# Gated outputs laid by token tile, and output products run between the gated steps, in a one-core decoder layer

## The reference

```
def hybrid_mixer(u, w_in, w_a2, b_a, b_f, g_gla, w_out):
    ...
    o_fox = fox_attention(fq.reshape(shp), fk.reshape(shp), fv.reshape(shp), log_f)
    ...
    o_gla = gla_chunked(...)          # o_intra + o_inter, per chunk of 64 tokens
    o_gla = rmsnorm(o_gla, g_gla.reshape(GLA_HEADS, GLA_HEAD_V)).reshape(B, S, GLA_VW)
    o_gla = o_gla * jax.nn.silu(gr)
    return jnp.concatenate([o_fox, o_gla], axis=-1) @ w_out
```

## Time and profile before

| | |
|---|---|
| median of 3 runs | 1203.12 us (1202.19 to 1206.01) |
| time of the profiled execution | 1202.4 us |
| its span, first to last instruction | 1200.7 us |
| TensorE busy | 1162.8 us, 97% |
| VectorE, ScalarE, GpSimd busy | 30%, 37%, 39% |
| mean granted clock of TensorE | 0.994 |

### The profile page before, as it was taken

The page is one execution under the profiler, slowest core; times in us unless marked ns, Lnnn a source line. Parts: engine busy times, 40 slices in busy tenths (PEclk is TensorE's granted clock), DMA queues, the critical chain, the costliest instruction groups (busy, mean ns, idle before and its releaser), DMA issues.

```text
span 1200.7 us, 14983 instructions
## 1 busy us (share of the span) xinstructions
PE 1162.8 (97%) x5565; PEld 963.0 (80%) x5565; DVE 355.6 (30%) x713; ACT 445.9 (37%) x728; POOL 472.7 (39%) x216
## 2 busy tenths in 40 slices
PE   8999999999999999999899999799999999999998
PEld 6888888888888778788678878678888888888886
DVE  3131221310006264655546104516213122130003
ACT  5232232322126455454535534425523223232213
POOL 2344354354442542222224753122543434435441
PEclk9999999999999999999999999899999999999999
DMA  6232323232322222111223442022332333323233
GB/s 197 88 105 87 105 87 105 88 105 88 105 90 69 88 88 71 53 53 54 71 70 117 146 142 88 18 71 71 93 101 94 98 97 95 100 93 104 90 102 109
DMA packets 83835, 110.91 MB, mean 92 GB/s; under 512 B 8718, under 2 KB 53836, under 8 KB 83788
## 3 DMA queue, kind: packets, MB, share of 16 engines
q1 hardware_dynamic: 83696, 110.24, 28.1%
q10 hardware_dynamic: 92, 0.02, 0.0%
HBM read 108.14 MB, written 2.10 MB: 92 GB/s over the span
## 4 chain that ended last, share of the span: by engine, by line
PE 67%; issue 19%; POOL 8%; DVE 4%; ACT 1%; DMA 1%; SPq 0%; POOLq 0%; DVEq 0%; ACTq 0%
PE bank L1397 22%; PE bank L1401 22%; PE bank L1398 22%; POOL w_lo L566 7%; DVE h L1050 1%; DVE tmp L1039 1%; DMA raw<-in_ffn_w_gu 1%; ACT w_hi L622 0%; POOL q_hi L604 0%; POOL q_lo L604 0%; DVE pt_lo L1170 0%; DVE xl L1002 0%; PE bank L1418 0%; PE bank L1421 0%; DVE smax L1144 0%
## 5 line engine op out<-in xcount | busy, mean ns | idle before, releaser
L566 POOL TENSOR_TENSOR w_lo<-raw,w_hi 128x1024 fp32r<-128x1024 f32 x193 | 461.5, 2403 | 707.5 <-ACT w_hi L622 695.2
L1397 PE MATMUL bank<-xh,w_hi 128*128 128x512 f32 (+1 forms) x920 | 353.3, 384 | 5.2 <-POOL w_lo L566 2.6
L1401 PE MATMUL bank<-xl,w_hi 128*128 128x512 f32 (+1 forms) x920 | 351.8, 382 | 0.0
L1398 PE MATMUL bank<-xh,w_lo 128*128 128x512 f32 (+1 forms) x920 | 351.7, 382 | 0.0
L622 ACT ACTIVATE w_hi<-raw 128x1024 fp32r<-128x1024 f32 x196 | 204.5, 1056 | 361.3 <-DMA raw<-in_ffn_w_down 169.3
L1397 PEld LDWEIGHTS bank<-xh,w_hi 128*128 128x128 f32 x920 | 173.0, 188 | 40.3 <-issue 3.9
L1401 PEld LDWEIGHTS bank<-xl,w_hi 128*128 128x128 f32 x920 | 173.1, 188 | 33.9
L1398 PEld LDWEIGHTS bank<-xh,w_lo 128*128 128x128 f32 x920 | 173.2, 188 | 32.2
L1397 PE MATMUL bank<-w_hi,mid_hi 128*128 128x512 f32 x352 | 137.3, 390 | 0.0
L1398 PE MATMUL bank<-w_hi,mid_lo 128*128 128x512 f32 x352 | 137.0, 389 | 0.0
L1401 PE MATMUL bank<-w_lo,mid_hi 128*128 128x512 f32 x352 | 137.0, 389 | 0.0
(11 more groups left out here) (227 smaller groups left out, 1168.6 us busy)
## 6 DMA issues: line engine op xcount, KB each, us to landing
raw<-in_ffn_w_gu SPq DMA_DIRECT2D x176, 256.0 KB, 2.9
raw<-in_ffn_w_down SPq DMA_DIRECT2D x88, 256.0 KB, 2.8
raw<-in_mix_w_in SPq DMA_DIRECT2D x48, 256.0 KB, 2.8
raw<-in_mem_w_kv SPq DMA_DIRECT2D x32, 256.0 KB, 3.1
raw<-in_mix_w_out SPq DMA_DIRECT2D x16, 256.0 KB, 2.8
raw<-in_mem_w_q SPq DMA_DIRECT2D x16, 256.0 KB, 3.0
raw<-in_mem_w_o SPq DMA_DIRECT2D x16, 256.0 KB, 2.9
h<-in_x SPq DMA_DIRECT2D x4, 512.0 KB, 5.3
```

What stands on the lines that cost most here:

```text
L566: gp.tensor_tensor(w_lo[:, n % SLOTS, :], raw[:, n % SLOTS, :], w_hi[:, n % SLOTS, :].bitcast(F32), ALU.subtract).then_inc(lo_ready, 1)
L1397: pe.matmul(dst, w[0], x[0], start=start, stop=False, skip_group_check=loose)
L1398: pe.matmul(dst, w[1], x[0], start=False, stop=False, skip_group_check=loose)
L1401: return pe.matmul(dst, w[0], x[1], start=False, stop=stop, skip_group_check=loose)
```

## The change

- The gated outputs of token tile m, all four heads, go to one bank (`gla_tile(m)`: bank 6 for even m, 7 for odd), and are squared and copied tile by tile inside the loop. Banks 4 and 5 are free from the start.
- The products with the state are cut in two: heads 0 and 2, then, after a wait for them (even_done), heads 1 and 3.
- FoX products of token tile 0 run earlier: block 0 ahead of the last FoX output, blocks 1 to 3 between the gated steps, three products at a time. Those of token tile 1 stay behind the steps.
- The key turns move ahead of the last FoX output, and their saving with them. The warm-up product is gone.
- Head sums are made per token: the squares of a head and tile are the weights, one column of ones is streamed, and the results are 16 columns of bank 0. Root and reciprocal work on 128 x 16. The spread makes four products of 128 columns a head in place of one of 512.

```
+            def square(m):
+                act.wait_ge(o_done, m + 1)
+                act.activation(tmp[:, :, m * P:(m + 1) * P], gla_tile(m), ACT.Square).then_inc(gsq, 1)
...
-                rms_root(tmp[:, 3, :], bank[0][:, :], GLA_V).then_inc(groot, 1)
+                rms_root(g_root[:, :], bank[0][:, 0:GLA_H * TC], GLA_V).then_inc(groot, 1)
...
+                def copy(m):
+                    dve.wait_ge(gsq, m + 1)
+                    dve.tensor_copy(o_sb[:, :, m * P:(m + 1) * P], gla_tile(m)).then_inc(gcopy, 1)
...
                     step(2 * m - 1)
                     step(2 * m)
-                dve.wait_ge(mem_root_s, 1)
-                dve.reciprocal(mem_rinv[:, :], mem_root[:, :]).then_inc(mem_inv, 1)
+                    if m == 2:
+                        dve.wait_ge(mem_root_s, 1)
+                        dve.reciprocal(mem_rinv[:, :], mem_root[:, :]).then_inc(mem_inv, 1)
+                    copy(m - 1)
+                copy(TC - 1)
...
-                dve.reciprocal(tmp[:, 3, :], tmp[:, 3, :]).then_inc(ginv, 1)
+                dve.reciprocal(g_rinv[:, :], g_root[:, :]).then_inc(ginv, 1)
...
+                    if phase == FOX and k == len(units) + late:
+                        fox_rows_out(0, 0)
+                        turn_ke()
...
+            def fox_rows_out(c, t, half=(0, 1)):
+
+                pe.wait_ge(y_l, 2 * c + 2)
+                free = {}
+                if c == 0:
+                    free = {0: (in_tmp, 13), 1: (in_tmp, 14)} if t == 0 else {2: (gcopy, 3), 3: (gcopy, 4)}
+                rows_block(1, B_OUT + c, fox_rows(c), c == 0, free=free, ms=tuple(2 * t + i for i in half), used=False)
...
+                    from_state(m, 0).then_inc(even_done, 1)
+
+                def from_state(m, e):
+
                     for n in (2 * m, 2 * m + 1):
                         if n:
                             tok = slice(n * CHUNK, (n + 1) * CHUNK)
-                            for hd in range(GLA_H):
+                            part = slice(n % 2 * CHUNK, (n % 2 + 1) * CHUNK)
+                            for hd in (e, e + 2):
                                 c, r, cols = head(hd)
-                                last = pe.matmul(bank[4 + hd][:, tok], state[r, n - 1, cols], gq[r, c, tok],
+                                last = pe.matmul(gla_tile(m)[:, hd, part], state[r, n - 1, cols], gq[r, c, tok],
                                                  start=False, stop=n % 2 == 1, skip_group_check=True)
...
+                def odd_outputs(m):
+
+                    pe.wait_ge(even_done, m + 1)
+                    from_state(m, 1).then_inc(o_done, 1)
+
+                def sums(m):
+
+                    pe.wait_ge(gsq, m + 1)
+                    for hd in range(GLA_H):
+                        last = pe.matmul(bank[0][:, hd * TC + m:hd * TC + m + 1], tmp[:, hd, m * P:(m + 1) * P],
+                                         ones[:, 0:1], start=hd == m == 0, stop=True, skip_group_check=True)
+                    return last
+
+                def spread_head(hd):
+                    if hd >= 2:
+                        pe.wait_ge(gfactor, hd - 1)
+                    for t in range(TC):
+                        last = pe.matmul(bank[1 - hd % 2][:, t * P:(t + 1) * P],
+                                         g_rinv[:, hd * TC + t:hd * TC + t + 1].to_broadcast([P, P]), ident[:, :],
+                                         start=True, stop=True)
+                    last.then_inc(gspread, 1)
+
...
-                pe.wait_ge(y_l, Y_FOX)
-                warm_up(bank[2], 1)
                 scores(0)
                 chunk_state(0)
                 for m in range(TC):
...
                         scores(m + 1)
                         chunk_state(2 * m + 1)
                         chunk_state(2 * m + 2)
+                        fox_rows_out(m + 1, 0, (0,))
                     outputs(m)
+                    if m + 1 < TC:
+                        fox_rows_out(m + 1, 0, (1,))
+                    else:
+                        for j in range(TC - 1):
+                            sums(j)
+                    odd_outputs(m)
...
-                pe.wait_ge(y_l, Y_FOX)
-                fox_out(0)
-                fox_out(1)
-                fox_out(2)
-                sums().then_inc(gstat, 1)
                 mem_turn(0)
-                fox_out(3)
-                fox_out(4)
+                sums(TC - 1).then_inc(gstat, 1)
+                fox_rows_out(0, 1)
+                fox_rows_out(1, 1)
                 pe.wait_ge(ginv, 1)
                 spread_head(0)
                 spread_head(1)
-                fox_out(5)
+                fox_rows_out(2, 1)
                 mem_turn(1)
-                fox_out(6)
                 spread_head(2)
                 spread_head(3)
-                fox_out(7)
+                fox_rows_out(3, 1)
```

More of the change, by code:

```diff
@@ L58 @@
 LEAD = 3
-SUM_ROWS = P // GLA_H
 TAU = 16.0
@@ L369, in build @@
         st_ready = sem("st_ready")
+        even_done = sem("even_done")
         o_done = sem("o_done")
@@ L884, in gla @@
                 act.preload_act_table(ACT.Sqrt)
+                act.wait_ge(in_hi, 20)
+                square(0)
                 act.wait_ge(mem_landed, 16 * MC)
@@ L891, in gla @@
                 rms_root(mem_root[:, :], mem_ms[:, :], D).then_inc(mem_root_s, 1)
+                square(1)
                 act.wait_ge(mem_inv, 1)
@@ L895, in gla @@
                                    scale=mem_rinv[:, t:t + 1]).then_inc(mem_normed, 1)
-                act.wait_ge(o_done, TC)
-                for hd in range(GLA_H):
-                    act.activation(tmp[:, hd, :], bank[4 + hd][:, :], ACT.Square).then_inc(gsq, 1)
+                    square(2 + t)
                 def mem_hi_chunks(cs):
@@ L1733, in fox_rows, with turn_ke @@
                 return fox_hi[:, c, :], fox_lo[:, c, :]
+            def fox_rows_out(c, t, half=(0, 1)):
[4 more added lines that the diff above has]
+                rows_block(1, B_OUT + c, fox_rows(c), c == 0, free=free, ms=tuple(2 * t + i for i in half), used=False)
+            def turn_ke():
+                pe.wait_ge(gdec, 3)
+                pe.wait_ge(expd, N_FOX)
+                for t in range(2):
+                    for j in range(4):
+                        m, c = 2 * t + j // 2, j % 2
+                        last = pe.transpose(bank[t][:, j * P:(j + 1) * P], gke[:, c, m * P:(m + 1) * P],
+                                            ident[:, :])
+                    last.then_inc(ke_turned, 1)
             def gla():
@@ L1820, in mem_turn @@
                             last.then_inc(mem_turned, 1)
-                def fox_out(q):
-                    c, t = q // 2, q % 2
-                    free = {2 * t + half: (gcopy, q * 2 + half + 1) for half in range(2)} if c == 0 else {}
-                    rows_block(1, B_OUT + c, fox_rows(c), c == 0, free=free, ms=(2 * t, 2 * t + 1), used=False)
-                def sums():
-                    for hd in range(GLA_H):
-                        pe.wait_ge(gsq, hd + 1)
-                        rows = slice(SUM_ROWS * hd, SUM_ROWS * (hd + 1))
-                        last = pe.matmul(bank[0][rows, :], ones[:, 0:SUM_ROWS], tmp[:, hd, :],
-                                         start=True, stop=True)
-                    return last
-                def spread_head(hd):
-                    if hd >= 2:
-                        pe.wait_ge(gfactor, hd - 1)
-                    row = SUM_ROWS * hd
-                    pe.matmul(bank[1 - hd % 2][:, :], ident[:, row:row + 1].to_broadcast([P, P]), tmp[:, 3, :],
-                              start=True, stop=True).then_inc(gspread, 1)
-                pe.wait_ge(y_l, Y_FOX)
-                fox_out(0)
-                fox_out(1)
-                fox_out(2)
-                sums().then_inc(gstat, 1)
                 mem_turn(0)
-                fox_out(3)
-                fox_out(4)
+                sums(TC - 1).then_inc(gstat, 1)
+                fox_rows_out(0, 1)
+                fox_rows_out(1, 1)
                 pe.wait_ge(ginv, 1)
```

30 lines of the change are left out of this document (14 added, 16 removed).

## The result

| | before | after |
|---|---|---|
| median of 5 runs each | 1203.24 us (1202.19 to 1206.01) | 1208.86 us (1207.32 to 1210.66) |
| profiled execution: time, span | 1202.4, 1200.7 us | 1207.51, 1205.8 us |
| mean granted clock of TensorE | 0.994 | 0.992 |

The ratio is 1.0043, 95% interval 1.0026 to 1.006. The kernel became 5.6 us slower, where +1.6 was forecast, and its median lies just outside the range. Ratios go by the means of the runs; where runs fall into two groups, the median can stand elsewhere, so both are given.

A forecast was written before the change was run, and what follows sets the result against it. TensorE was taken as the bound, working 1162.8 of 1200.7 us. Gains of 5.0 us against costs of 6.6 gave net +1.6 us on the median of 1203.12, so 1204.7 us, range 1200.8 to 1208.4.

The forecast's parts named there:

- The front, the waits: Front, end of gated steps, before spreads: waits go, gaining 2.7, 1.7 and 0.6 us; new mask wait of 0.7 us.
- State products and changes of mode: Gated steps: one-half state products at 0.107 us a step cost 3.0 us; 64-row/128-row switches cost 1.1 us.
- Head sums: Behind squares of gated outputs: 32 weight loads at 0.107 us, 3.4 us less the old 1.0, cost 2.4 us.
- the wait for ginv: Before the spreads: reciprocal on 16 columns instead of 512, with 12 products covering it, removes the wait, gain 0.6 us.
- Sum of the work: Whole stretch: gains 5.0, costs 6.6, net +1.6 us; second token half at 614.5 instead of 612.9; chance 0.47.
- The clock falls in the sums: Rival, behind last tile's inner products: mostly weight loads bring half clock, +3.3 us, 1206.4; second fall 1208.1; chance 0.30.

The follow-up runs named there:

- The reorderings alone: Kernel before with key turns and memory turns moved earlier, no warm-up product, old-form sums behind six FoX products: 1198.16 us, ratio 0.9961.
- fourth experiment: Kernel before with only the order of its state products changed: heads 0 and 2, then 1 and 3; 1203.98 us, ratio 1.0011.
- the four lines above: Stretch times of changed kernel, its repeat, sums directly behind turns, sums behind six FoX products: 47.42, 45.87, 45.86, 44.30 us with 10.24, 6.83, 6.83, 3.42 at half clock.
- sixth experiment: Kernel before with only the one-column head sums and their root, reciprocal and spreads: 1205.36 us, ratio 1.0014.
- third experiment: Changed kernel with the old head sums, root, reciprocal and spreads put back: 1202.55 us, ratio 1.0001.
- tenth: Changed kernel with all 32 sum instructions in one row behind the memory turns and six FoX products: 1204.56 us, ratio 1.0019.
- first: Changed kernel with one 512-column dummy product behind each of the three early groups of head sums: 1215.36 us, ratio 1.0072, in two groups.
- seventh: Changed kernel with nine FoX products of token tile 1 moved among the early sums: 1206.7 us, ratio 1.0043, in groups.
- ninth: Changed kernel with five full products of FoX data, result unused, behind each of the three early head sums: 1213.93 us, ratio 1.0074.

## Why the prediction was wrong, step by step

- **The front, the waits.** Right: scores(1) at 578.73 with 0.69 us on the mask (579 and 0.7 forecast), no wait behind the steps nor ahead of the spreads. The reorderings alone confirm that these gains are real: 3.6 us in the stretch, 5 in the time.
- **State products and changes of mode.** Steps of 0.107 as forecast for eight in a row (1.03 us with a mode change), no pairs. From scores(1) to the memory turns the changed kernel takes 603.14 - 578.73 = 24.4 us; less 24 sums (2.6), 18 FoX products (4.1) and what the half clock cost (0.6) that is 17.1, where the kernel before takes 593.24 - 580.33 = 12.9. So these two terms are 4.2 together, 3.0 + 1.1 forecast. Right. In the kernel before the same split costs 1.5 (fourth experiment), because its halves overlap; here FoX products or sums stand between them. Only the odd products of two tiles meet the next scores, and little is saved by it:

```profile
589.41 0.77 PE L1832 MATMUL bank<-gq,state 64*128 64x64 f32 x5
...
590.35 0.66 PE L1790 MATMUL bank<-gq,gk 64*128 64x128 f32 x5
590.85 1.13 PE L1806 MATMUL bank<-gv,gla_a 64*128 64x256 f32 x8
```

Eight state products and eight scores take 590.85 - 589.41 = 1.44 us, against 1.03 and, in the kernel before, 0.51 (587.35 to 587.86) apart.

- **Head sums.** 0.109 us a load, 3.49 for 32: right as work, and +1.7 to +2.2 us alone with their spreads (2.5 forecast, less the 0.6 of the wait for ginv, is 1.9). The Trainium skill's price for a product of one column (TensorEngine Tiling (Array Packing), section Instruction Overhead), some 0.8 us in all as the prediction's estimate, doesn't hold with full weight loads: the trace has 3.49.
- **Sum of the work.** 42.3 us for the stretch without the half clock (47.42 - 5.1), or 42.7 by the four lines above; 42.4 forecast (614.5 - 572.07). Right.
- **The clock: this is the step that failed.** "The clock falls in the sums" was a rival with 0.30, priced at +3.3 us (1206.4) with a fall of 3.41 us, or 1208.1 with another; the sum itself put the clock at nothing. It fell in both profiled executions, for 10.24 and 6.83 us, and all eleven runs of the changed kernel lie above 1207.1 us. The place was right (598 to 608 was named); what failed is the chance, and the size of one fall. The argument against it was that the earlier trace rows keep 1.00 through all gated steps and two long waits. That was one execution, of a list without one-column sums; the sixth experiment has 0.50 from 594.75 behind the same long wait, so there was less room than it seemed. And the price took a fall for one piece of 3.41 us, as in the earlier trace rows. A fall lasted over whatever followed: odd products, turns, sums, and the twelve FoX products behind them, which took 5.27 us (606.46 to 611.73) instead of some 2.8.

What is shown: the one-column sums are needed for the loss (third experiment); their work is some 2 us of it (sixth); the rest comes from their place, since the same instructions behind six dense products cost 2.9 to 3.9 us less (tenth); and it passes through the granted clock, for the stretch becomes longer with each microsecond at half clock and with nothing else (the four lines), and one program differs from itself by 10 us (first). The tenth stands at 1.0019, +2.3 us, about where the prediction was, with a short fall left.

What stays open: how much emptiness, over how long, makes the clock fall. The kernel before has 14.49 us of gated steps without a full product at 1.00, its state products in pairs; the third experiment has 5.3 us of state products in rows of one half, products within the tile and turns (595.29 to 600.62) at 1.00; in the first the fall began after 3.8 us without a full product (596.52 to 600.29), 0.6 us into the one-column sums. So by these executions length alone isn't it, but unpaired half-array products, turns and one-column sums stood together wherever the clock fell in the sums, and no run parts them. Nor was it settled why in the first, seventh and ninth experiments some executions of the same program seem to escape the fall.

## What to carry to other kernels

When a change puts products that leave the array nearly empty (one streamed column, half the rows without pairs, turns) next to one another, don't take the clock from a trace without them: TensorE was busy throughout and the clock fell, and one execution at 1.00 in the kernel before had not told it. Try the order first: the same instructions with dense work ahead of such a row, and not among it, were worth some 3 us here. Compare such orders by the stretch itself and its time at half clock, since falls elsewhere come and go from run to run. And before changing a layout to fill waits, try the reordering alone, which took 3.6 us off the stretch and was 5 us faster.

## What was not expected of the hardware

- The clock fell with no idle time of TensorE ahead of it for over 20 us (busy 18.92 of 18.92 and 4.26 of 4.26 us in the windows after). The Trainium skill (TensorE: Matmul & The Clock Gate, section HAM oscillation — how this bites in real kernels) puts such falls down to gaps in which TensorE is idle. Here no gap was needed.
- Once down, the clock stayed down through dense work: 17.07 us with ten products of data and twelve FoX products in it (ninth), 20.48 with three dummy products and the same twelve (first), and in the changed kernel through twelve FoX products in a row from 606.46.
- A state product starts together with a score product on the other row half, a pair each 0.11 us (fourth experiment, from 587.11), as two state products of different halves do. The score at 586.89 even starts ahead of three state products that stand before it in the list.
